# Three vectors on another queue, modulation units behind the product, and one group of row sums moved up, in a fused decoder layer

## The reference

```python
c_act = silu(c)
mod = (c_act @ w_ada + b_ada).reshape(3, 3, 1024)        # nine vectors: shift, scale, gate of three sub-layers
h = rms_norm(x, g1) * (1 + mod[0, 1]) + mod[0, 0]
x = x + 0.5 * mod[0, 2] * ((silu(h @ Wg) * (h @ Wu)) @ w_out1)      # FFN 1, hidden width 2816
h = rms_norm(x, gmix) * (1 + mod[1, 1]) + mod[1, 0]
x = x + mod[1, 2] * (mixers(h @ w_mix_in) @ w_mix_out)              # pooling and gated spatial mixers
h = rms_norm(x, g2) * (1 + mod[2, 1]) + mod[2, 0]
x = x + 0.5 * mod[2, 2] * ((silu(h @ Vg) * (h @ Vu)) @ w_out2)      # FFN 2
y = rms_norm(x, gfin)
```

## Time and profile before

| | us |
|---|---|
| median of 3 runs | 911.21 |
| lowest and highest | 909.74, 917.93 |
| the profiled execution, device time | 916.22 |
| its span in the trace | 914.1 |
| TensorE busy in the span | 870.5 |
| VectorE, ScalarE, GpSimd busy | 586.0, 331.6, 49.6 |

### The profile page before, as it was taken

One profiled execution on the slowest core, in us unless ns is written; L12 is line 12 of the kernel. 1 busy time (PEld: TensorE's weight loads), 2 busy tenths in 40 slices (PEclk: granted clock), 3 DMA queues, 4 the chain that ended last, 5 costly groups with the idle time before them and its releaser, 6 DMA issues.

```text
span 914.1 us, 13700 instructions
## 1 busy us (share of the span) xinstructions
PE 870.5 (95%) x5290; PEld 750.8 (82%) x5290; DVE 586.0 (64%) x897; ACT 331.6 (36%) x434; POOL 49.6 (5%) x45
## 2 busy tenths in 40 slices
PE   4798999999999999998999998899999999999997
PEld 3676888888888888896887897799988899999886
DVE  2559777777776565637454559888833388886443
ACT  5231222222222222224323335556621166665233
POOL 0000000000000000002160022000000000010000
PEclk9799999999999999999999999999999999999999
DMA  9947766666654655444432224366543656653322
GB/s 284 282 128 231 207 186 190 191 191 189 188 173 137 191 161 168 141 124 127 127 84 72 75 58 116 80 167 159 124 127 95 138 132 166 174 141 107 95 64 92
DMA packets 219483, 134.44 MB, mean 147 GB/s; under 512 B 5560, under 2 KB 214572, under 8 KB 219436
## 3 DMA queue, kind: packets, MB, share of 16 engines
q1 hardware_dynamic: 216384, 128.47, 49.4%
q0 software_dynamic: 2880, 5.24, 3.7%
q10 hardware_dynamic: 172, 0.06, 0.0%
HBM read 126.41 MB, written 2.10 MB: 141 GB/s over the span
## 4 chain that ended last, share of the span: by engine, by line
PE 89%; DVE 6%; ACT 2%; DMA 1%; issue 1%; ACTq 0%; DVEq 0%
PE ps L1551 21%; PE ps L1552 21%; PE ps L1553 21%; PE ps L1916 7%; PE ps L1912 7%; PE ps L1914 7%; DVE h_lo L1007 1%; PE ps L1742 1%; PE ps L1805 1%; PE ps L1806 1%; PE ps L1807 1%; DMA vrow<-in_pool_scale_dram 1%; DVE ada_acc L1051 1%; DVE sw_lo_a L1434 1%; ACT work L652 0%
## 5 line engine op out<-in xcount | busy, mean ns | idle before, releaser
L1551 PE MATMUL ps<-h_hi,w_split 128*128 128x512 f32 (+1 forms) x464 | 184.1, 397 | 15.8 <-DVE h_lo L1007 11.7
L1553 PE MATMUL ps<-h_hi,w_split 128*128 128x512 f32 (+1 forms) x464 | 182.2, 393 | 0.0
L1552 PE MATMUL ps<-h_lo,w_split 128*128 128x512 f32 (+1 forms) x464 | 181.8, 392 | 0.0
L954 DVE TENSOR_TENSOR w_split<-w_raw,w_split 128x2048 fp32r<-128x2048 f32 (+1 forms) x44 | 91.0, 2067 | 86.9 <-ACT w_split L598 86.9
L1551 PEld LDWEIGHTS ps<-h_hi,w_split 128*128 128x128 f32 x464 | 89.0, 192 | 38.5 <-DVE h_lo L1007 10.2
L598 ACT CAST w_split<-w_raw 128x2048 fp32r<-128x2048 f32 (+1 forms) x45 | 77.2, 1716 | 93.2 <-PE ps L1553 70.5
L1553 PEld LDWEIGHTS ps<-h_hi,w_split 128*128 128x128 f32 x464 | 89.1, 192 | 19.3
L1552 PEld LDWEIGHTS ps<-h_lo,w_split 128*128 128x128 f32 x464 | 89.0, 192 | 18.4
L1051 DVE SCALAR_TENSOR_TENSOR ada_acc<-ada_raw,c_act,ada_acc 128x256 f32<-128x256 f32 x196 | 95.0, 485 | 7.3 <-DMA ada_raw<-in_w_ada_dram 0.3
L1912 PE MATMUL ps<-sums_hi,sw_hi 128*128 128x256 f32 x320 | 89.9, 281 | 4.2 <-ACT ev L864 3.7
L1914 PE MATMUL ps<-sums_lo,sw_hi 128*128 128x256 f32 x320 | 90.1, 282 | 0.0
(11 more groups left out here) (187 smaller groups left out, 1555.8 us busy)
## 6 DMA issues: line engine op xcount, KB each, us to landing
ada_raw<-in_w_ada_dram SPq DMA_DIRECT2D x56, 512.0 KB, 3.6
sw_raw<-in_ffn_w_in_dram SPq DMA_DIRECT2D x100, 256.0 KB, 4.2
w_raw<-in_ffn_w_in_dram SPq DMA_DIRECT2D x48, 512.0 KB, 6.0
ada_first<-in_w_ada_dram SPq DMA_DIRECT2D x16, 512.0 KB, 7.5
w_raw<-in_ffn_w_out_dram SPq DMA_DIRECT2D x16, 384.0 KB, 5.0
w_raw<-in_w_mix_in_dram SPq DMA_DIRECT2D x12, 512.0 KB, 4.3
sw_raw<-in_ffn_w_out_dram SPq DMA_DIRECT2D x16, 384.0 KB, 4.1
w_raw<-in_ffn_w_out_dram SPq DMA_DIRECT2D x16, 320.0 KB, 4.3
```

Of the source, the lines that this page charges most:

```text
L954: nc.vector.tensor_tensor(w_lo[s][:, 0:n], w_raw[s][:, 0:n], w_hi[s][:, 0:n].bitcast(F32), ALU.subtract).then_inc(lo_ready, 1)
L1551: nc.tensor.matmul(dst, w_h, a_h, start=start, stop=False)
L1552: nc.tensor.matmul(dst, w_h, a_l, start=False, stop=False)
L1553: return nc.tensor.matmul(dst, w_l, a_h, start=False, stop=stop)
```

## The change

The change has three parts, and no instruction is added or taken away. (1) The loads of c, b_ada and g1 go from ScalarE's queue to the head of SyncE's, ahead of x. (2) In FFN 1's up steps the modulation unit stands behind product, split and `a_lo` in steps 0 to 19, and ahead of them in steps 20 and 21. (3) Tile 7's row sums move from behind tile 5's products for both chunks to between the two chunks' products.

```diff
@@ SyncE @@
+            def load_vec(name, v):
+                n = v.shape[-1] // P
+                sp.dma_start(vrow[rows[name]:rows[name] + n, :], v.rearrange("a (k p) -> (a k) p", p=P))\
+                  .then_inc(vec_full, 16)
+
+            load_vec("c", c)
+            load_vec("b_ada", b_ada)
+            load_vec("g1", norm_ffn1_g)
             for t in range(NT):
                 load_x(t)
@@ ScalarE @@
-            load_vec("c", c)
-            load_vec("b_ada", b_ada)
-            load_vec("g1", norm_ffn1_g)
             load_vec("gmix", norm_mix_g)
@@ VectorE @@
                 first = isinstance(jn, int) and jn == 0
-                if ada and not first:
+                early = isinstance(j, int) and j >= KF - 2
+                if ada and early:
                     ada_unit(j)
 ...
-                if ada and first:
+                if ada and not early:
                     ada_unit(j)
@@ TensorE @@
             for k in range(3, KD - 1):
                 first_rows_of(k)
-                for s in range(2):
-                    first_products(k - 1, s)
-            first_rows_of(KD - 1)
+                first_products(k - 1, 0)
+                if k == KD - 2:
+                    first_rows_of(KD - 1)
+                first_products(k - 1, 1)
```

## The result

The changed kernel takes **1011.5 us** (median of 6 runs, 1010.2 to 1014.7), the kernel before 911.3 (6 runs, 909.7 to 917.9). The ratio is 1.109, with a 95% interval of 1.106 to 1.112: 100 us slower. The profiled execution took 1010.9 us, its span is 1008.9; that of before took 916.2 and spanned 914.1, so between the two profiles there are 94.8 us.

What follows compares the result with a forecast made beforehand. TensorE was taken as the bound, busy 870.5 of 914.1 us. Part 2's +95.3, part 1's -3 and part 3's -1 gave +91.3 us on 916.2, so 1007.5 profiled and 1003 for a median, range 982 to 1024.

Steps and rivals of the forecast that it cites:

- the ring: Up steps: unit's end, next chunk's load, cast, split, `a_lo` and next unit form a closed loop; 16.4 us, TensorE needs 11.2.
- unit's end to cast: Up steps: from a unit's last multiply-add to the start of the cast of the chunk requested behind it, 7.7 us.
- one turn: Up steps: the sum from one unit's end to the next, 16.4 us, so each step costs 5.2 us more.
- start of chunk 4, with parts 1 and 3: Early up steps: 2.5 us left of chunk 3's gain, plus 4 us from the vectors and row sums.
- chunks 5 to 21: Up steps: 17 turns at 5.2 us more each, +88.4 us.
- chunk 22: End of the up steps: starts 20.0 us after chunk 21, not 11.2, as unit 19 stands right ahead of unit 20; +8.8 us.
- chunk 23's split: Behind unit 21 on VectorE: the split adds about 0.6 us.
- The start: Kernel start and tile 7: earlier vectors, landing at 5 to 8 us, give -3 us; earlier row sums give -1.0 us.
- The shift from profile to median: Whole kernel: the profile before lay 5.0 us over the median, so 1007.5 profiled became 1003 for a median.
- The ring is closed: Up steps: its rival, ring not closed, had 5%: steps stay at 11.2 us and the kernel takes 901.5 us, faster.
- TensorE at half clock: Up steps, rival, 4%: half clock becomes the bound, chunks last up to 20.5 us, up to +70 us, 1073.
- The ring doesn't turn faster: Up steps: its rival, a faster ring from weights landing sooner, had 10%: 1 us less for each turn gives 986.

Runs made afterwards that it cites:

- the second profile of before: The kernel before, unchanged, profiled a second time: this execution took 914.4 us with a span of 912.4 us.
- eight more matmuls a step: The changed kernel with eight more 128x512 matmuls behind each chunk from 4 to 21, into a PSUM bank nobody reads then: 1012.5 us.
- the vectors alone: The kernel before with only part 1, c, b_ada and g1 at the head of SyncE's queue: 911.4 us, ratio 0.998.
- the row sums alone: The kernel before with only part 3, tile 7's row sums between the two chunks' products of tile 5: 911.9 us, ratio 0.999.
- the order alone: The kernel before with only SyncE's queue reordered, each chunk's weights one unit further ahead: 911.3 us, ratio 1.000.
- the units alone: The kernel before with only part 2, modulation units behind product and split in steps 0 to 19: 1015.1 us, ratio 1.114.

## Why the prediction was right, and its sizes

1003 was forecast, in a range of 982 to 1024, and 1011.5 measured. The mechanism is shown: the loss is part 2's alone, it goes away when only SyncE's order is changed, it shrinks by what is cut out of the ring, and more work on TensorE doesn't lengthen it. By the steps of the prediction, in times between the two profiles:

| step | forecast | measured |
|---|---|---|
| unit's end to cast | 7.7 us | 7.7, mean of 17 turns |
| one turn | 16.4 | 16.45 |
| start of chunk 4, with parts 1 and 3 | -2.5 - 4 = -6.5 | -7.3 |
| chunks 5 to 21 | +88.4 | +89.2 |
| chunk 22 | +8.8 | +9.8 |
| end of chunk 22 (TensorE goes on with the sums, 301.51 and 395.04) | no more than that | +1.8 |
| chunk 23's split | +0.6 | none seen |
| everything behind | 0 | +1.3 |
| profile to profile | +91.3 | +94.8 |

- **Chunk 4.** The -7.3 has a gain at the start that was larger than forecast and a gain of part 2 that was smaller. The first silu came 5.65 us earlier (below), so 1.6 us are left for part 2, where 2.5 were forecast. Unit 1 ended its last multiply-add at 68.78 + 3.61 = 72.39 and the cast of chunk 4 started at 80.67, 8.3 us later; the prediction took the 7.46 of the trace before. It also put chunk 4's start before at 92.35, and the row says 92.21. That the two errors nearly cancel is luck.
- **Chunk 22.** Two small terms were missed. Unit 19 ends at 365.39 + 3.62 = 369.01 and unit 20 at 372.93 + 2.05 = 374.98, 5.97 apart (5.72 forecast), and the cast starts 7.44 behind that (6.70 forecast). And I had the half clock cost nothing, since the ring leaves room for it. That holds for the 17 turns, but chunk 22 stands outside them: it starts behind a wait of 8.1 us, runs at half clock at first, and takes 9.5 us (385.50 to 395.04) where it took 7.7, with nothing behind it to hide that.
- **Everything behind.** The last 1.3 us were not followed up; no stage is named for them.
- **The start.** -4.0 was forecast for parts 1 and 3. Between the two profiles it is -5.65 (first silu 61.36 to 55.71), but the first profile of before was a late one: the five profiles without these parts lie between 59.03 and 61.36, the four with both between 55.64 and 57.49. Between kernels that differ by these parts alone the medians say 3.6 and 3.9. The vectors landed at 4.8 us, just below my 5 to 8. ScalarE's last square of x ends at 17.30 us before and at 12.49 in the changed kernel, 4.8 us earlier, as much as the vectors did; the first product gains only 3.9 (24.58 to 20.69). The Trainium skill's rule that the prediction named, that another queue saves issue time only, would have made it 0 or worse. The trace doesn't bear that out for these small loads: the last vector was issued 1.1 us earlier (3.18 to 2.10) and TensorE's wait for the vectors ended 4.8 us earlier (3.5 against the second profile of before). That b_ada's rows no longer come through x's traffic is the likely reason; which of the three vectors matters was not tried.
- **The shift from profile to median failed**, and it is the largest error: 5.0 of the 8.5 us by which 1003 was short. I took the 5.0 us by which the profile of before lay over its median as a thing that the changed kernel would have too. It has not: its profiled execution (1010.9) and its median (1011.5) agree. Up to 3.8 us of such a difference is the matmuls' pitch in the up steps, as the second profile of before shows, and a loop whose turn is set by VectorE and a DMA doesn't feel TensorE's pitch: it didn't feel eight more matmuls a step either. The rest of the 5.0 is not accounted for. Without the shift the forecast would have been 1007.5.
- **The rivals.** The ring is closed. TensorE at half clock is no bound (the eight matmuls). The ring doesn't turn faster: landing took 6.2 us in the turn shown, with the same three transfers beside each other, and the mean of 17 turns from unit's end to cast is the 7.7 us of the sum. The Trainium skill's rule ("TensorE: Matmul & The Clock Gate", "HAM oscillation") that a wait for data in each tile makes each tile start at half clock agrees with the trace for 14 of the 18 chunks: 0.43 us from matmul to matmul, from 85.75 on behind the wait that ended at 84.95. It doesn't for the other four, behind waits of 2.3 to 3.4 us. The cost was hidden in the turns and showed only at chunk 22.

## What to carry to other kernels

Before work is moved on one engine, follow what its completion releases: here a unit's end gates a transfer, and behind that transfer, in the same queue, stand the weights that the very next instruction wants. The same move was worth 100 us of loss with one order of the queue and 6 to 7 us of gain with the other. A ring of that kind is told from a lack of time on an engine by its idle time: the engine that everybody waits for is idle itself for half of each turn (7.8 of 16.45 us here). And a difference between a profile and the median may belong to a stretch that the change takes off the critical path; it is not carried over unseen.

## What the runs showed of the hardware

- **Two pitches at full clock.** In the up steps, matmuls of 128x512 followed each other at 229 ns in some stretches and at 233 ns in others, at the same granted clock of 1.0. A stretch without an interruption kept its pitch, however long: 18 chunks at 233 (11.20 us each) in the first profile of before and with the vectors alone, 18 at 229 (10.99) in the second, with the row sums alone and with the order alone. Behind an interruption the pitch could be the other one. In the first profile of before it was 229 ahead of the wait at 79.40, 233 behind it, and 229 again behind the sums at 301.51. In the changed kernel, which waits ahead of each chunk, three chunks went on at 233 (from 205.4, 253.2 and 304.3) and the others at 229. A return from half clock is not needed: with the units alone the pitch went from 229 to 233 at 61.98, behind a wait of 0.23 us and at a granted clock of 1.0 on both sides. What picks it stays open.
- **Small loads in heavy traffic.** TensorE's wait for the seven vectors, 58 KB in all, ended at 8.1 to 9.7 us in the six profiles in which they were issued beside x, and at 4.8 us in the five in which c, b_ada (72 rows) and g1 went ahead of x. x itself started 1.2 us later and cost TensorE only 0.4 to 0.7 us of waiting.
